# Decay gates of gated linear attention kept feature-major, logarithms two heads at a time, chunk sums by scans on VectorE

## The chip, the cores and the metric

One core of one Trainium2 chip runs the whole program. The metric is the time of one execution on the device in microseconds (us), as the median of three runs. Beside it one execution was taken by the hardware profiler; its span is the time from the first to the last instruction of the profile.

## What is computed

The kernel computes two two-layer transformer blocks on 256 tokens of width 1024 in float32. The first has a forgetting-gate attention layer, a latent attention layer and two squared-relu feed-forward layers; the second has a gated linear attention layer (GLA), a short-convolution layer and two convolutional feed-forward layers. The change touches only the GLA mixer, and in it only the decay gates:

```python
def gla_mixer(h, w_in, w_gate_up, b_gate, head_norm_g, w_out):   # 4 heads, key dim 128, value dim 256
    q, k, v, g, a_low = split(h @ w_in)                           # a_low: 16 columns
    log_a = log_sigmoid(a_low @ w_gate_up + b_gate) / 16          # 512 gates for each token
    bcum = cumsum(log_a, inside chunks of 64 tokens)
    q_in = q * 128 ** -0.5 * exp(bcum)
    k_in = k * exp(-bcum)
    k_dec = k * exp(b_last - bcum)                                # b_last: bcum at the chunk's end
    # masked scores q_in k_in inside a chunk, k_dec carries the state to the next chunk
```

The kernel has log_sigmoid(z) as min(z, 0) - ln(1 + exp(min(z, -z))).

## The kernel before, in words

**Matrix products.** Activations stand feature-major (features on partitions, 256 tokens in the free direction). Every weight matrix arrives from memory in chunks of 256 columns into four raw slots (`w_raw`). A chunk is two halves of 128 columns. For each half ScalarE rounds the raw weights into `w_hi` (line 1344), VectorE computes the remainder `w_lo` (line 1753), and TensorE makes 24 matrix products with them (lines 782 to 784, or 814 to 816 where tokens are to stand on partitions). A helper called `prep` does this on ScalarE and on VectorE, three halves ahead of the half that TensorE is at. `w_hi` and `w_lo` have room for four halves, so ScalarE's `prep` waits until TensorE has finished the half that lies four before. TensorE waits for `w_lo` before each half (`split_ready`), and in the GV stage before each pair of halves, since each token block there uses both halves of a chunk.

**Order.** Each engine executes its own list in the written order; semaphores tie the lists together. The stages around the change are GA (the 16 low-rank gate columns), GQK (8 halves, queries and keys), GV (8 token blocks over 8 halves, values), GG (8 halves, output gate) and GO. What is not a matrix product of a stage is written between the halves at fixed places: "if n == 3" is after the evacuation of half 3 of the stage.

**The decay gates before.** Behind GQK half 2 TensorE makes the gate product token-major, one 512-column product for each block of 128 tokens (line 1208). On VectorE, behind GQK half 3, for each token block the bias is added (line 2159, from a copy of the bias on all partitions, `g_bias`) and min(z, -z) is taken (line 2160). ScalarE, at GQK step 4 between two `prep`s, takes exp and then ln(1 + .) of all 1024 columns at once (lines 1627 and 1629). VectorE behind GQK half 6 forms the logarithm of the decay (line 2165). Behind token block 0 of GV TensorE forms the sums inside chunks, feature-major, by eight float32 products with a triangular matrix (`gla_cum`, line 1216); they land in the two PSUM banks `score`. ScalarE makes exp of them and of their negatives (lines 1635 and 1638). VectorE forms the differences to the chunk ends (lines 2180 to 2187), ScalarE their exponentials (lines 1652 and 1653), and VectorE multiplies keys and queries by them (lines 2192 to 2202).

VectorE evacuates each half of GQK from PSUM with one operation (`scaled`, line 1931). ScalarE evacuates the GV blocks in pairs (line 1646).

Lines in the profile are lines of the kernel before.

Of the kernel before, what the change touches and what calls it, by code (L numbers as in the profile page):

```python
# [78 lines left out]
for _name, _n in [("mix0", 8), ("ffn0", 8), ("kv", 8), ("mix1", 8), ("ffn1", 8), ("final1", 8), ("mix2", 8),  # L79
                  ("ffn2", 8), ("mix3", 8), ("ffn3", 8), ("final2", 8), ("kv_a", 2), ("q_a", 3), ("head", 8),  # L80
                  ("sc_conv", 24), ("conv0", 132), ("conv1", 132)]:
    VEC[_name] = N_VEC
    N_VEC += _n
# [7 lines left out]
for _name, _n in [("ones", 128), ("ident", 128), ("mask", 256), ("tri_chunk", 128), ("cos", 256),  # L91
                  ("sin", 256), ("tile_mask", 128), ("pick", FOX_H),
                  ("head_row", 3 * 32 + P), ("eps", 1)]:
    CON[_name] = N_CON
    N_CON += _n


def shape_constants():

    con = np.zeros((P, N_CON), np.float32)  # L100
    at = lambda name, n: con[:, CON[name]:CON[name] + n]
    i = np.arange(P)
    at("ones", 128)[:] = 1.0
    at("ident", 128)[:] = np.eye(P)

    at("mask", 256)[:, 128:] = np.where(i[None, :] <= i[:, None], 0.0, MASKED)

    same = (i[:, None] // GLA_C) == (i[None, :] // GLA_C)
    upto = i[:, None] <= i[None, :]
    at("tri_chunk", 128)[:] = np.where(same & upto, 1.0 / GATE_TAU, 0.0)  # L110
# [12 lines left out]
    return con  # L123


def build(nc, io):
    ctx = ExitStack()
    with ctx:
# [93 lines left out]
        g_z = sb("g_z", [P, TT, 512])  # L222
        g_e = sb("g_e", [P, TT, 512])
# [17 lines left out]
        g_bias = sb("g_bias", [P, 512])  # L241
# [26 lines left out]
        tri_chunk = con[:, CON["tri_chunk"]:CON["tri_chunk"] + 128]  # L268
# [245 lines left out]
        def _(sp):  # L514
# [80 lines left out]
            sp.dma_start(g_bias[:], io["gla_b_gate_2"][0:1, :].partition_broadcast(P)).then_inc(gla_small_landed, 16)  # L595
# [52 lines left out]
        def _(pool):  # L648
# [94 lines left out]
            for h in range(GLA_H):  # L743
                pool.wait_ge(gla_act, 15 + 4 * h)
                nc.gpsimd.tensor_tensor(tmp_of(2 * h), tmp_of(2 * h), tmp_of(2 * h + 1), ALU.add).then_inc(head_sq, 1)
# [12 lines left out]
        def _(pe):  # L758
# [469 lines left out]
            def gla_scores(t):  # L1228

                pe.wait_ge(gla_dve, 11)  # L1230
# [15 lines left out]
            def gla_out(n):  # L1246

                h = n // 2
                e = slice(n * P, (n + 1) * P)
                bank_ = gla_bank[n % 4]  # L1250
                if n == 0:
                    pe.wait_ge(act_evac, AE["GV"] + 8)
                    pe.wait_ge(gla_act, 11)
                    pe.wait_ge(gla_dve, 13)
                if n >= 4:
                    pe.wait_ge(gla_act, 11 + 2 * (n - 4) + 2)
                nc.tensor.matmul(bank_[:, 0:T], g_v[:, 0, e], g_sT[:, h, 0:2, :], start=True, stop=False)
                step(nc.tensor.matmul(bank_[:, P:T], g_v[:, 1, e], g_sT[:, h, 2, :], start=False, stop=True))

            def gla_stat():  # L1260

                pe.wait_ge(gla_act, 27)
                for h in range(GLA_H):
                    pe.wait_ge(head_sq, h + 1)
                    last = nc.tensor.matmul(misc[:, 0:T], head_row[:, 32 * (3 - h):32 * (3 - h) + P], tmp_of(2 * h), start=h == 0,
                                            stop=h == GLA_H - 1)
                step(last)

            def gla_spread():

                pe.wait_ge(gla_dve, 15)
# [56 lines left out]
        def _(act):  # L1328
# [292 lines left out]
            for n in range(8):  # L1621
# [3 lines left out]
                if n == 4:  # L1625
                    act.wait_ge(gla_dve, 2)
                    step(nc.scalar.activation(g_e[:], g_e[:], ACT.Exp))
                    act.wait_ge(gla_act, 1)
                    step(nc.scalar.activation(g_e[:], g_e[:], ACT.Ln, bias=1.0))
            prep(C0["GV"], 0)  # L1630
            for g in range(2):
                act.wait_ge(gla_pe, 3 + g)
                hs = slice(2 * g, 2 * g + 2)
                v = score[g][:].rearrange("p (h t) -> p h t", h=2)
                step(nc.scalar.activation(g_eb[:, hs, :], v, ACT.Exp))
                v = v.rearrange("p h (t c s) -> p h t c s", t=TT, c=2)
                for c in range(2):
                    step(nc.scalar.activation(key_tiles(c)[:, hs], v[:, :, :, c, :], ACT.Exp, scale=-1.0))
            for n in range(8):
# [10 lines left out]
                if n == 1:  # L1650
                    act.wait_ge(gla_dve, 6)
                    step(nc.scalar.activation(g_kk[:, :, K_X:K_X + P], g_kk[:, :, K_X:K_X + P], ACT.Exp))
                    step(nc.scalar.activation(far_keys(), far_keys(), ACT.Exp))
# [3 lines left out]
                if n == 6:  # L1657
                    act.wait_ge(gla_pe, 7)
# [10 lines left out]
            for n in range(8):  # L1669
                if n < 7:  # L1670
                    prep(C0["GG"] + n // 2, n % 2)
                if n in (1, 2):
                    for m in range(4 * (n - 1), 4 * (n - 1) + 4):
                        act.wait_ge(gla_pe, 8 + m)
                        if m == 0:
                            act.wait_ge(gla_dve, 11)
                        step(nc.scalar.activation(g_o[:, m, :], gla_bank[m % 4][:, 0:T], ACT.Copy, scale=gain("head", m)))
                        step(nc.scalar.activation(tmp_of(m), gla_bank[m % 4][:, 0:T], ACT.Square))
                if n == 3:
                    act.wait_ge(gla_dve, 14)  # L1680
# [64 lines left out]
        def _(dve):  # L1745
# [421 lines left out]
            def near_scores(t):  # L2167
                dve.wait_ge(gla_zeroed, 1)
                dve.wait_ge(gla_pe, 5 + t)
# [3 lines left out]
            for n in range(8):  # L2173
                prep(C0["GV"] + n // 2, n % 2)
                if n == 0:
                    for g in range(2):
                        dve.wait_ge(gla_act, 5 + 3 * g)
# [21 lines left out]
                if n == 3:  # L2199
                    dve.wait_ge(gla_act, 10)  # L2200
# [13 lines left out]
            def head_norm(m):  # L2214

                dve.wait_ge(gla_pe, 17 + m // 2)
# [7 lines left out]
            for n in range(8):  # L2224
# [6 lines left out]
                if n == 3:  # L2231
                    dve.wait_ge(gla_act, 28)
# [6 lines left out]
                if n == 2:  # L2239
                    dve.wait_ge(gla_pe, 16)  # L2240
# [69 lines left out]
            "ffn_w_up", "ffn_w_down", "gla_w_in_2", "gla_b_gate_2", "gla_w_out_2", "sc_w_in_2",  # L2310
# [35 lines left out]
```

## Time and profile before

| what | value |
|---|---|
| median of 3 runs | 1117.34 us (1117.2 to 1117.8) |
| the profiled execution | 1117.06 us |
| its span | 1115.3 us |
| TensorE busy in the span | 1109.2 us (99%) |
| VectorE busy | 851.9 us (76%) |
| ScalarE busy | 664.5 us (60%) |
| GpSimd busy | 252.9 us (23%) |
| DMA queue of the weights | 201.90 MB, 56.0% of 16 engines' span |

In the profile PE is TensorE's matrix products and PEld its weight loads, DVE is VectorE, ACT ScalarE, POOL GpSimd, SP the engine that issues the transfers. Matrix products overlap: each is shown with its whole latency, so the time that one costs is the distance between the starts of neighbours. In a timeline a line holds the start, the duration, the engine, the source line, the operation, what it writes and reads, how many instructions were merged into it, and in brackets the idle time before it with what ended that.

### The profile page before, as it was taken

Reading aid. Unit: us, or ns where it says so; the run is one execution under the profiler, and the core shown is the slowest. Engines: PE = TensorE matmul, PEld = TensorE weight load, DVE = VectorE, ACT = ScalarE, POOL = GpSimd, SP = SyncE. Lnnn points to the kernel's source line nnn. Section 1 sums busy time; section 2 is a strip of 40 time slices with the busy share of each in tenths; the row PEclk is TensorE's granted clock in tenths of the full one; section 3 lists DMA queues with packets and bytes.
Section 4 is the critical chain, followed back from the end, with each engine's and each line's share of the span. In section 5 each row is a group of like instructions: output and inputs, shape, how many; then the busy total and the mean of one; then the engine's idle time right before and its main releaser. Section 6 shows DMA issues by size and latency. Waiting matters only on the chain.

```text
span 1115.3 us, 26109 instructions
## 1 busy us (share of the span) xinstructions
PE 1109.2 (99%) x9634; PEld 1093.9 (98%) x9634; DVE 851.9 (76%) x1373; ACT 664.5 (60%) x1113; POOL 252.9 (23%) x248
## 2 busy tenths in 40 slices
PE   9999999999999999999999999999999999999998
PEld 9999999999998999999999999999999999999998
DVE  7866877666686977756577699999658888999854
ACT  7666666545577656644466566666455456666544
POOL 0002300001140500011200364544211034444421
PEclk9999999999999999999999999999999999999999
DMA  9533755555652765565464455654666565655461
GB/s 336 191 130 114 227 188 188 190 196 179 170 180 77 223 193 188 178 202 193 150 195 146 152 188 166 205 196 141 207 205 226 173 216 169 201 200 179 150 213 62
DMA packets 206799, 203.02 MB, mean 182 GB/s; under 512 B 9824, under 2 KB 204896, under 8 KB 206736
## 3 DMA queue, kind: packets, MB, share of 16 engines
q1 hardware_dynamic: 206592, 201.90, 56.0%
q8 instruction: 42, 0.69, 0.3%
q10 hardware_dynamic: 144, 0.26, 0.1%
q14 instruction: 21, 0.17, 0.0%
HBM read 201.10 MB, written 1.05 MB: 181 GB/s over the span
## 4 chain that ended last, share of the span: by engine, by line
PE 99%; DVE 0%; issue 0%; ACT 0%; DVEq 0%
PE gemm L782 29%; PE gemm L784 29%; PE gemm L783 29%; PE gemm L814 2%; PE gemm L815 1%; PE gemm L816 1%; PE gemm L791 1%; PE gemm L793 1%; PE gemm L792 1%; PE score L1015 1%; PE gemm L1027 1%; PE score L1147 0%; PE misc L1052 0%; PE misc L844 0%; PE gemm L1163 0%; PE score L1235 0%
## 5 line engine op out<-in xcount | busy, mean ns | idle before, releaser
L1753 DVE TENSOR_TENSOR w_lo<-w_raw,w_hi 128x1024 fp32r<-128x1024 f32 (+2 forms) x401 | 478.9, 1200 | 140.7 <-ACT w_hi L1344 138.8
L1344 ACT CAST w_hi<-w_raw 128x1024 fp32r<-128x1024 f32 (+2 forms) x401 | 400.4, 1004 | 141.8 <-PE gemm L784 136.4
L782 PE MATMUL gemm<-act_a,w_hi 128*128 128x256 f32 (+1 forms) x1688 | 466.6, 276 | 0.0
L784 PE MATMUL gemm<-act_a,w_lo 128*128 128x256 f32 (+1 forms) x1688 | 464.6, 275 | 0.0
L783 PE MATMUL gemm<-act_a,w_hi 128*128 128x256 f32 (+1 forms) x1688 | 464.5, 275 | 0.0
L782 PEld LDWEIGHTS gemm<-act_a,w_hi 128*128 128x128 f32 (+1 forms) x1688 | 316.2, 187 | 2.1 <-issue 1.8
L783 PEld LDWEIGHTS gemm<-act_a,w_hi 128*128 128x128 f32 (+1 forms) x1688 | 316.2, 187 | 0.3
L784 PEld LDWEIGHTS gemm<-act_a,w_lo 128*128 128x128 f32 (+1 forms) x1688 | 316.1, 187 | 0.2
L782 PE MATMUL gemm<-hid,w_hi 128*128 128x256 f32 x864 | 238.2, 276 | 0.0
L784 PE MATMUL gemm<-hid,w_lo 128*128 128x256 f32 x864 | 237.7, 275 | 0.0
L783 PE MATMUL gemm<-hid,w_hi 128*128 128x256 f32 x864 | 237.7, 275 | 0.0
L783 PEld LDWEIGHTS gemm<-hid,w_hi 128*128 128x128 f32 x864 | 162.2, 188 | 0.1
L782 PEld LDWEIGHTS gemm<-hid,w_hi 128*128 128x128 f32 x864 | 162.2, 188 | 0.1
L784 PEld LDWEIGHTS gemm<-hid,w_lo 128*128 128x128 f32 x864 | 162.2, 188 | 0.0
L661 POOL TENSOR_TENSOR sqt<-x 128x256 f32<-128x256 f32 x47 | 54.0, 1149 | 274.7 <-DVE x L1810 190.1
L684 POOL TENSOR_TENSOR tmp<-tmp,tmp 128x256 f32<-128x256 f32 x44 | 67.9, 1543 | 119.5 <-DVE tmp L1885 119.5
L1433 ACT ACTIVATE tmp<-tmp,vec 128x256 f32<-128x256 f32 x88 | 44.9, 511 | 77.7 <-DVE tmp L1870 72.6
L1394 ACT ACTIVATE tmp<-gemm 128x256 f32<-128x256 f32 x64 | 24.6, 384 | 59.3 <-PE gemm L784 59.3
L782 PE MATMUL gemm<-act_b,w_hi 128*128 128x256 f32 x216 | 59.6, 276 | 0.0
L784 PE MATMUL gemm<-act_b,w_lo 128*128 128x256 f32 x216 | 59.4, 275 | 0.0
L783 PE MATMUL gemm<-act_b,w_hi 128*128 128x256 f32 x216 | 59.4, 275 | 0.0
L1885 DVE SCALAR_TENSOR_TENSOR tmp<-tmp,vec,tmp 128x254 f32<-128x254 f32 x88 | 47.7, 542 | 12.7 <-DVE tmp L1882 1.8
(302 smaller groups left out, 1427.7 us busy)
## 6 DMA issues: line engine op xcount, KB each, us to landing
w_raw<-in_ffn_w_up SPq DMA_DIRECT2D x76, 1024.0 KB, 5.2
w_raw<-in_ffn_w_down SPq DMA_DIRECT2D x32, 1024.0 KB, 5.2
w_raw<-in_gla_w_in SPq DMA_DIRECT2D x12, 1024.0 KB, 5.1
w_raw<-in_ffn_w_down SPq DMA_DIRECT2D x16, 768.0 KB, 4.5
w_raw<-in_sc_w_in SPq DMA_DIRECT2D x12, 1024.0 KB, 5.2
w_raw<-in_fox_w_in SPq DMA_DIRECT2D x10, 1024.0 KB, 7.3
w_raw<-in_ffn_w_down SPq DMA_DIRECT2D x16, 640.0 KB, 4.2
w_raw<-in_fox_w_out SPq DMA_DIRECT2D x4, 1024.0 KB, 5.1
```

The costliest lines, as they stand in the source:

```text
L661: nc.gpsimd.tensor_tensor(sqt[:], tile, tile, ALU.mult).then_inc(pool_sq, 1)
L684: nc.gpsimd.tensor_tensor(y, y, tmp2[:, n % 2, :], ALU.mult).then_inc(gated_ready, 1)
L782: nc.tensor.matmul(ps, wh[:, k, cols], act[:, k0 + k, 0, :], start=start and k == 0, stop=False)
L783: nc.tensor.matmul(ps, wh[:, k, cols], act[:, k0 + k, 1, :], start=False, stop=False)
L784: last = nc.tensor.matmul(ps, wl[:, k, cols], act[:, k0 + k, 0, :], start=False, stop=stop and k == nk - 1)
L791: nc.tensor.matmul(ps, wh, act[:, k, 0, :], start=k == 0, stop=False)
L814: nc.tensor.matmul(ps, act[:, k, 0, tok], wh(k), start=k == 0, stop=False)
L1344: nc.scalar.copy(split_half(w_hi, nc_, nj), raw_half(nc_, nj)).then_inc(w_hi_ready, 1)
L1394: nc.scalar.activation(tmp[:, n % 4, :], bank_of(stage, n)[:, 0:T], ACT.Relu).then_inc(act_evac, 1)
L1433: nc.scalar.activation(tmp[:, n % 4, :], tmp2[:, 2 + n % 2, :], ACT.Copy, scale=w).then_inc(tap_ready, 1)
L1753: nc.vector.tensor_tensor(split_half(w_lo, nc_, nj), raw_half(nc_, nj), split_half(w_hi, nc_, nj).bitcast(F32), ALU.subtract).then_inc(w_l ...
L1885: nc.vector.scalar_tensor_tensor(out=y[:, 2:T], in0=u[:, 0:T - 2], scalar=w0, in1=y[:, 2:T], op0=ALU.mult, op1=ALU.add).then_inc(conv_done, 1)
```

## The change

The gate product is made feature-major: four products of 256 tokens, one for each head, into the two `score` banks. The bias is then a column of `vec` and no longer a broadcast copy, and its transfer goes. Minimum and exp and ln are taken for two heads at a time, so ScalarE's order becomes exp, ln, exp, ln on 512 columns each. The triangular matrix, its eight products and `gla_cum` go; in their place VectorE runs one scan for each head over 256 tokens. The scan multiplies the running sum by a row `chunk_start` that is 0 at the first token of each chunk and 1 elsewhere, which restarts it. The division by 16 goes into the scale of the later exponentials. Those now read `g_e` in SBUF in place of the `score` banks. The VectorE work is spread: decay logarithm and scan of head 0 behind GQK half 5, scan of head 1 and decay logarithm of heads 2 and 3 behind half 6, scans of heads 2 and 3 behind half 7. The constants' tensor grows by 128 columns and `vec` by 4. All other hunks only renumber semaphore values.

```diff
@@ TensorE
-                pe.wait_ge(gla_small_landed, 32)
-                for t in range(TT):
-                    r = slice(32 * t, 32 * t + GATE_RANK)
-                    step(nc.tensor.matmul(score[t][:, 0:512], g_aT[r, t * P:(t + 1) * P], g_up[r, :], start=True, stop=True))
-
-            def gla_cum():
-
-                pe.wait_ge(gla_dve, 4)
-                for g in range(2):
-                    for h in range(2 * g, 2 * g + 2):
-                        for t in range(TT):
-                            last = nc.tensor.matmul(score[g][:, (h % 2) * T + t * P:(h % 2) * T + (t + 1) * P],
-                                                    g_z[:, t, h * P:(h + 1) * P], tri_chunk, start=True, stop=True)
-                    step(last)
+                pe.wait_ge(gla_small_landed, 16)
+                for h in range(GLA_H):
+                    r = slice(32 * (h % 2), 32 * (h % 2) + GATE_RANK)
+                    last = nc.tensor.matmul(score[h % 2][:, h // 2 * T:h // 2 * T + T], g_up[r, h * P:(h + 1) * P], g_aT[r, :],
+                                            start=True, stop=True)
+                    if h >= 2:
+                        step(last)
...
                 token_half("GV", n, act_a, act_evac, AE["GV"])
-                if n == 0:
-                    gla_cum()
@@ ScalarE
                 if n == 4:
-                    act.wait_ge(gla_dve, 2)
-                    step(nc.scalar.activation(g_e[:], g_e[:], ACT.Exp))
-                    act.wait_ge(gla_act, 1)
-                    step(nc.scalar.activation(g_e[:], g_e[:], ACT.Ln, bias=1.0))
+                    for g in range(2):
+                        hs = slice(2 * g, 2 * g + 2)
+                        act.wait_ge(gla_dve, 1 + g)
+                        step(nc.scalar.activation(g_e[:, hs, :], g_e[:, hs, :], ACT.Exp))
+                        act.wait_ge(gla_act, 1 + 2 * g)
+                        step(nc.scalar.activation(g_e[:, hs, :], g_e[:, hs, :], ACT.Ln, bias=1.0))
             prep(C0["GV"], 0)
             for g in range(2):
-                act.wait_ge(gla_pe, 3 + g)
+                act.wait_ge(gla_dve, 5 + 3 * g)
                 hs = slice(2 * g, 2 * g + 2)
-                v = score[g][:].rearrange("p (h t) -> p h t", h=2)
-                step(nc.scalar.activation(g_eb[:, hs, :], v, ACT.Exp))
+                v = g_e[:, hs, :]
+                step(nc.scalar.activation(g_eb[:, hs, :], v, ACT.Exp, scale=1.0 / GATE_TAU))
@@ VectorE
             def bcum(g):
-                return score[g][:].rearrange("p (c s) -> p c s", s=GLA_C)
+                return g_e[:, 2 * g:2 * g + 2, :].rearrange("p h (c s) -> p (h c) s", s=GLA_C)
+
+            def log_decay(g):
+                hs = slice(2 * g, 2 * g + 2)
+                step(nc.vector.scalar_tensor_tensor(out=g_z[:, hs, :], in0=g_z[:, hs, :], scalar=0.0, in1=g_e[:, hs, :],
+                                                    op0=ALU.min, op1=ALU.subtract), wait=True)
+
+            def chunk_sums(h):
+                step(nc.vector.tensor_tensor_scan(g_e[:, h, :], chunk_start, g_z[:, h, :], 0.0, ALU.mult, ALU.add))
...
                 if n == 3:
-                    for t in range(TT):
-                        dve.wait_ge(gla_pe, 1 + t)
-                        dve.wait_ge(gla_small_landed, 32)
-                        link(nc.vector.tensor_tensor(g_z[:, t, :], score[t][:], g_bias[:], ALU.add))
-                        step(nc.vector.scalar_tensor_tensor(out=g_e[:, t, :], in0=g_z[:, t, :], scalar=-1.0, in1=g_z[:, t, :],
-                                                            op0=ALU.mult, op1=ALU.min))
+                    for h in range(GLA_H):
+                        dve.wait_ge(gla_pe, 1 + h % 2)
+                        last = nc.vector.tensor_scalar(g_z[:, h, :], score[h % 2][:, h // 2 * T:h // 2 * T + T], gain("gate", h), None,
+                                                       ALU.add)
+                        if h % 2:
+                            link(last)
+                            hs = slice(h - 1, h + 1)
+                            step(nc.vector.scalar_tensor_tensor(out=g_e[:, hs, :], in0=g_z[:, hs, :], scalar=-1.0, in1=g_z[:, hs, :],
+                                                                op0=ALU.mult, op1=ALU.min))
+                if n == 5:
+                    dve.wait_ge(gla_act, 2)
+                    log_decay(0)
+                    chunk_sums(0)
                 if n == 6:
-                    dve.wait_ge(gla_act, 2)
-                    for t in range(TT):
-                        step(nc.vector.scalar_tensor_tensor(out=g_z[:, t, :], in0=g_z[:, t, :], scalar=0.0, in1=g_e[:, t, :],
-                                                            op0=ALU.min, op1=ALU.subtract))
+                    chunk_sums(1)
+                    dve.wait_ge(gla_act, 4)
+                    log_decay(1)
+                if n == 7:
+                    chunk_sums(2)
+                    chunk_sums(3)
```

Here `link` waits for the end of the instruction before, `step` counts one up on a semaphore, and `step(..., wait=True)` also waits for it.

## Rows read from the trace of the kernel before

**Rows 1.** The page: engines' busy time, and TensorE's granted clock in 40 slices.

```profile
PE 1109.2 (99%) x9634; PEld 1093.9 (98%) x9634; DVE 851.9 (76%) x1373; ACT 664.5 (60%) x1113; POOL 252.9 (23%) x248
...
PEclk9999999999999999999999999999999999999999
```

**Rows 2.** The waits of TensorE, first of two: us, times, longest.

```profile
PE misc L1052 <- DVE f_cum L1962: 1.2, 1, 1.2
```

**Rows 3.** Timeline of TensorE: gate product, GV token blocks and chunk sums.

```profile
565.03 1.13 PE L1208 MATMUL score<-g_up,g_aT 16*128 16x512 f32 x4
566.09 0.39 PE L782 MATMUL gemm<-act_a,w_hi 128*128 128x256 f32 x1
...
579.85 0.28 PE L814 MATMUL gemm<-w_hi,act_a 128*128 128x256 f32 x1
...
582.57 1.95 PE L1216 MATMUL score<-con,g_z 128*128 128x128 f32 x16
584.28 0.37 PE L814 MATMUL gemm<-w_hi,act_a 128*128 128x256 f32 x1
584.49 0.28 PE L815 MATMUL gemm<-w_hi,act_a 128*128 128x256 f32 x1
...
587.12 0.28 PE L814 MATMUL gemm<-w_hi,act_a 128*128 128x256 f32 x1
...
592.56 0.29 PE L814 MATMUL gemm<-w_hi,act_a 128*128 128x256 f32 x1
```

**Rows 4.** Timeline of VectorE in GQK, from the evacuation of half 3.

```profile
569.18 0.41 DVE L1931 TENSOR_TENSOR g_q<-gemm,rstd 128x256 f32<-128x256 f32 x1
569.52 0.68 DVE L2159 TENSOR_TENSOR g_z<-score,g_bias 128x512 f32<-128x512 f32 x1
570.23 0.69 DVE L2160 SCALAR_TENSOR_TENSOR g_e<-g_z 128x512 f32<-128x512 f32 x1
...
572.16 1.22 DVE L1753 TENSOR_TENSOR w_lo<-w_raw,w_hi 128x1024 fp32r<-128x1024 f32 x1
...
578.16 1.22 DVE L1753 TENSOR_TENSOR w_lo<-w_raw,w_hi 128x1024 fp32r<-128x1024 f32 x1
...
579.63 1.28 DVE L2165 SCALAR_TENSOR_TENSOR g_z<-g_z,g_e 128x512 f32<-128x512 f32 x2
```

**Rows 5.** Timeline of ScalarE at GQK step 4, and the rounding behind it.

```profile
570.24 1.28 ACT L1627 ACT_TABLE_LOAD   x1
572.28 1.06 ACT L1627 ACTIVATE g_e<-g_e 128x1024 f32<-128x1024 f32 x1 [0.76 <-DVE g_e L2160]
573.36 1.28 ACT L1629 ACT_TABLE_LOAD   x1
574.66 1.06 ACT L1629 ACTIVATE g_e<-g_e 128x1024 f32<-128x1024 f32 x1
575.62 2.93 ACT L1344 CAST w_hi<-w_raw 128x1024 fp32r<-128x1024 f32 x3
```

**Rows 6.** Timeline of VectorE in the first layer: a scan and its successor.

```profile
27.98 0.68 DVE L2017 TENSOR_TENSOR_SCAN f_exp<-con,f_z 16x256 f32<-16x256 f32 x1
28.59 0.38 DVE L1931 TENSOR_TENSOR f_q<-gemm,rstd 128x256 f32<-128x256 f32 x1
```

**Rows 7.** Timeline of VectorE in GV: first and last chunk-end operation, w_lo.

```profile
584.85 0.17 DVE L2180 COPY g_last<-score 128x8 f32<-128x8 f32 x1 [1.33 <-ACT g_kk L1638]
...
587.04 0.42 DVE L2187 TENSOR_TENSOR g_kk<-g_end,score 128x256 f32<-128x256 f32 x1
...
591.17 1.23 DVE L1753 TENSOR_TENSOR w_lo<-w_raw,w_hi 128x1024 fp32r<-128x1024 f32 x1 [0.16 <-ACT w_hi L1344]
```

**Rows 8.** Timeline of ScalarE in GV, step 1: exponential and next rounding.

```profile
589.04 0.64 ACT L1652 ACTIVATE g_kk<-g_kk 128x512 f32<-128x512 f32 x1
...
590.10 1.05 ACT L1344 CAST w_hi<-w_raw 128x1024 fp32r<-128x1024 f32 x1
```

**Rows 9.** The first matrix products of the program, by their source line (ns).

```profile
L1052 PE MATMUL misc<-f_cum x22: 283/415/579, 1.2 to 5.8; 128*128 128x256 f32 x22
```

More of the change, by code:

```diff
@@ L80 @@
                   ("ffn2", 8), ("mix3", 8), ("ffn3", 8), ("final2", 8), ("kv_a", 2), ("q_a", 3), ("head", 8),
-                  ("sc_conv", 24), ("conv0", 132), ("conv1", 132)]:
+                  ("sc_conv", 24), ("conv0", 132), ("conv1", 132), ("gate", GLA_H)]:
     VEC[_name] = N_VEC
@@ L90 @@
 N_CON = 0
-for _name, _n in [("ones", 128), ("ident", 128), ("mask", 256), ("tri_chunk", 128), ("cos", 256),
+for _name, _n in [("ones", 128), ("ident", 128), ("mask", 256), ("chunk_start", 256), ("cos", 256),
                   ("sin", 256), ("tile_mask", 128), ("pick", FOX_H),
@@ L106, in shape_constants @@
     at("mask", 256)[:, 128:] = np.where(i[None, :] <= i[:, None], 0.0, MASKED)
-    same = (i[:, None] // GLA_C) == (i[None, :] // GLA_C)
     upto = i[:, None] <= i[None, :]
-    at("tri_chunk", 128)[:] = np.where(same & upto, 1.0 / GATE_TAU, 0.0)
+    at("chunk_start", 256)[:] = np.where(np.arange(T) % GLA_C == 0, 0.0, 1.0)[None, :]
     at("tile_mask", 128)[:] = np.where(upto, 1.0, 0.0)
@@ L221, in build @@
         g_v = sb("g_v", [P, TT, D])
-        g_z = sb("g_z", [P, TT, 512])
-        g_e = sb("g_e", [P, TT, 512])
+        g_z = sb("g_z", [P, GLA_H, T])
+        g_e = sb("g_e", [P, GLA_H, T])
         g_eb = sb("g_eb", [P, GLA_H, T])
@@ L240, in build @@
         g_up = sb("g_up", [GATE_ROWS, 512])
-        g_bias = sb("g_bias", [P, 512])
         s_c = sb("s_c", [P, 2, T])
@@ L267, in build @@
         mask = con[:, CON["mask"]:CON["mask"] + 256]
-        tri_chunk = con[:, CON["tri_chunk"]:CON["tri_chunk"] + 128]
+        chunk_start = con[:, CON["chunk_start"]:CON["chunk_start"] + 256]
         cos_t = con[:, CON["cos"]:CON["cos"] + 256]
@@ L743, in _ @@
             for h in range(GLA_H):
-                pool.wait_ge(gla_act, 15 + 4 * h)
+                pool.wait_ge(gla_act, 17 + 4 * h)
                 nc.gpsimd.tensor_tensor(tmp_of(2 * h), tmp_of(2 * h), tmp_of(2 * h + 1), ALU.add).then_inc(head_sq, 1)
@@ L1228, in gla_scores @@
             def gla_scores(t):
-                pe.wait_ge(gla_dve, 11)
+                pe.wait_ge(gla_dve, 15)
                 for h in range(GLA_H):
@@ L1252, in gla_out @@
                     pe.wait_ge(act_evac, AE["GV"] + 8)
-                    pe.wait_ge(gla_act, 11)
-                    pe.wait_ge(gla_dve, 13)
+                    pe.wait_ge(gla_act, 13)
+                    pe.wait_ge(gla_dve, 17)
                 if n >= 4:
-                    pe.wait_ge(gla_act, 11 + 2 * (n - 4) + 2)
+                    pe.wait_ge(gla_act, 13 + 2 * (n - 4) + 2)
                 nc.tensor.matmul(bank_[:, 0:T], g_v[:, 0, e], g_sT[:, h, 0:2, :], start=True, stop=False)
@@ L1260, in gla_stat @@
             def gla_stat():
-                pe.wait_ge(gla_act, 27)
+                pe.wait_ge(gla_act, 29)
                 for h in range(GLA_H):
@@ L1269, in gla_spread @@
             def gla_spread():
-                pe.wait_ge(gla_dve, 15)
+                pe.wait_ge(gla_dve, 19)
                 for h in range(GLA_H):
@@ L1625, in _ @@
                 if n == 4:
-                    act.wait_ge(gla_dve, 2)
-                    step(nc.scalar.activation(g_e[:], g_e[:], ACT.Exp))
-                    act.wait_ge(gla_act, 1)
-                    step(nc.scalar.activation(g_e[:], g_e[:], ACT.Ln, bias=1.0))
+                    for g in range(2):
[4 more added lines that the diff above has]
+                        step(nc.scalar.activation(g_e[:, hs, :], g_e[:, hs, :], ACT.Ln, bias=1.0))
             prep(C0["GV"], 0)
             for g in range(2):
-                act.wait_ge(gla_pe, 3 + g)
+                act.wait_ge(gla_dve, 5 + 3 * g)
                 hs = slice(2 * g, 2 * g + 2)
-                v = score[g][:].rearrange("p (h t) -> p h t", h=2)
-                step(nc.scalar.activation(g_eb[:, hs, :], v, ACT.Exp))
+                v = g_e[:, hs, :]
+                step(nc.scalar.activation(g_eb[:, hs, :], v, ACT.Exp, scale=1.0 / GATE_TAU))
                 v = v.rearrange("p h (t c s) -> p h t c s", t=TT, c=2)
                 for c in range(2):
-                    step(nc.scalar.activation(key_tiles(c)[:, hs], v[:, :, :, c, :], ACT.Exp, scale=-1.0))
+                    step(nc.scalar.activation(key_tiles(c)[:, hs], v[:, :, :, c, :], ACT.Exp, scale=-1.0 / GATE_TAU))
             for n in range(8):
@@ L1650, in _ @@
                 if n == 1:
-                    act.wait_ge(gla_dve, 6)
-                    step(nc.scalar.activation(g_kk[:, :, K_X:K_X + P], g_kk[:, :, K_X:K_X + P], ACT.Exp))
-                    step(nc.scalar.activation(far_keys(), far_keys(), ACT.Exp))
+                    act.wait_ge(gla_dve, 10)
+                    step(nc.scalar.activation(g_kk[:, :, K_X:K_X + P], g_kk[:, :, K_X:K_X + P], ACT.Exp, scale=1.0 / GATE_TAU))
+                    step(nc.scalar.activation(far_keys(), far_keys(), ACT.Exp, scale=1.0 / GATE_TAU))
                 if n == 2:
@@ L1657, in _ @@
                 if n == 6:
-                    act.wait_ge(gla_pe, 7)
+                    act.wait_ge(gla_pe, 5)
                     act.wait_ge(gla_zeroed, 1)
@@ L1673, in _ @@
                     for m in range(4 * (n - 1), 4 * (n - 1) + 4):
-                        act.wait_ge(gla_pe, 8 + m)
+                        act.wait_ge(gla_pe, 6 + m)
                         if m == 0:
-                            act.wait_ge(gla_dve, 11)
+                            act.wait_ge(gla_dve, 15)
                         step(nc.scalar.activation(g_o[:, m, :], gla_bank[m % 4][:, 0:T], ACT.Copy, scale=gain("head", m)))
@@ L1679, in _ @@
                 if n == 3:
-                    act.wait_ge(gla_dve, 14)
+                    act.wait_ge(gla_dve, 18)
                     step(nc.scalar.activation(g_std, g_var, ACT.Sqrt))
@@ L2176, in _ @@
                     for g in range(2):
-                        dve.wait_ge(gla_act, 5 + 3 * g)
+                        dve.wait_ge(gla_act, 7 + 3 * g)
                         hs = slice(2 * g, 2 * g + 2)
@@ L2199, in _ @@
                 if n == 3:
-                    dve.wait_ge(gla_act, 10)
+                    dve.wait_ge(gla_act, 12)
                     step(nc.vector.tensor_tensor(g_kk[:, :, K_B:K_B + T], g_kk[:, :, K_B:K_B + T], g_k[:], ALU.mult))
@@ L2214, in head_norm @@
             def head_norm(m):
-                dve.wait_ge(gla_pe, 17 + m // 2)
+                dve.wait_ge(gla_pe, 15 + m // 2)
                 if m < KD - 1:
@@ L2231, in _ @@
                 if n == 3:
-                    dve.wait_ge(gla_act, 28)
+                    dve.wait_ge(gla_act, 30)
                     step(nc.vector.reciprocal(g_rec, g_std))
@@ L2239, in _ @@
                 if n == 2:
-                    dve.wait_ge(gla_pe, 16)
+                    dve.wait_ge(gla_pe, 14)
                     step(nc.vector.tensor_scalar(g_var, misc[:, 0:T], 1.0 / GLA_DV, EPS, ALU.mult, ALU.add))
```

7 lines of the change are left out of this document (3 added, 4 removed).

## The prediction

> **What bounds the kernel.** I read the page first: TensorE is busy 99% of the span, and its granted clock is full in every slice [rows 1]. Then the list of who waits for whom, for TensorE alone. It has only two entries, and the longer is 1.2 us at the very start [rows 2]. So TensorE sets the end, and a change can do only two things to the time: give TensorE more or less to do, or make it wait where it did not. The reader should see in the timelines how much it was from waiting in the region of the change. That is the distance from the moment when the second w_lo of a GV pair is finished to the moment when TensorE takes it. For halves 0 and 1 of GV the second remainder runs 578.16 to 579.38 [rows 4] and TensorE starts the block at 579.85 [rows 3]: 0.47 us to spare. For halves 4 and 5 it runs 591.17 to 592.40 [rows 7] and TensorE starts at 592.56 [rows 3]: 0.16 us to spare. Both pairs hang on a rounding that ScalarE does behind its exp and ln work. This is the place to cost with care.
>
> **TensorE's own work.** The sixteen records of the chunk sums begin at 582.57, and the next GV product at 584.28, 1.71 us later. The product behind that begins 0.21 later where neighbours elsewhere stand 0.113 apart (48 from 587.12 to 592.56, which is 5.44 / 48), so another 0.10 goes [rows 3]. Removing the sums gives **-1.81 us**.
>
> The gate product has 1024 columns before and after, as two products of 512 and then four of 256, each again two records. Now it takes 1.06 us to the next product [rows 3]. Four records of 512 columns in 1.06 us overlap in pairs: 128 columns cost 0.107 (1.71 / 16), so 512 would cost 0.43 alone, and four of them 1.71. The new form also alternates the two groups of rows, so I take no change. If it did not overlap it would cost 1.71, which is +0.65; if it overlapped better, 0.86, which is -0.20.
>
> **VectorE behind GQK half 3.** A 128x256 operation out of PSUM lasts 0.41 and lets the next start after 0.34; a 128x512 one lasts 0.69 [rows 4] and lets the next start after 0.61 (with the 0.03 of a link, 570.23 to 572.16 is twice 0.61 plus one 0.71). New: 0.34 + 0.41 + 0.03, then the minimum at 570.30, finished at 570.99; the second pair is done at 572.38, and the block takes 2.78 in place of 2.64. The +0.14 delays only the w_lo of the last GQK half, which TensorE takes some five microseconds later, and so costs nothing.
>
> **ScalarE at GQK step 4.** Here the cost arises. Before there is one table load (1.28) ahead of exp and one between exp and ln [rows 5]. With the order exp, ln, exp, ln there are four loads. The first is finished at 571.52, behind the first minimum (570.99), so exp of heads 0 and 1 starts at 571.54. A 128x512 activation lasts about 0.62 (0.64 in [rows 8]), and 0.02 lies on both sides of a load. One step exp, load, ln, load is 0.62 + 0.02 + 1.28 + 0.02 + 0.62 + 0.02 + 1.28 + 0.02 = 3.88. The second exp starts at 575.42 and the second ln at 577.36. The next rounding follows 0.53 behind it (589.04 to 590.10 is two such steps [rows 8]), at 577.89. It starts at 575.62 before. So the roundings of GV halves 0 to 3 come **2.27 us later**. In terms: two loads of 1.28, two more activation starts (4 x 0.62 - 2 x 1.06 = 0.36), 0.09 of gaps, less the 0.74 by which the first exp starts sooner. Three roundings take 2.93 [rows 5], 0.94 from start to start: half 0 is rounded by 578.94, half 1 by 579.88.
>
> **VectorE behind GQK half 5.** w_lo of half 0 starts at 578.96 and lets the next start after 1.14; the evacuation takes 0.34; then the decay logarithm, waited for to its end (0.69 + 0.03); then the first scan. The only scan in the trace, 16x256, lasts 0.68 and lets the next operation start after 0.61 [rows 6]. The same 256 columns on 128 partitions should cost the same, since evacuations of 16 and 128 partitions differ little; bounds are 0.34 (a plain 128x256 operation) and 1.22, twice the row of the scan; I take the row itself. w_lo of half 1 then starts at 578.96 + 1.14 + 0.34 + 0.72 + 0.61 = 581.77 and is finished at 582.99. TensorE is ready at 579.85 and starts at 583.01: it **waits 3.16 us**. The work that was put between the two remainders (0.72 + 0.61) makes 1.33 of it, the late rounding the rest, less the 0.47 that there was to spare.
>
> **The next pairs.** VectorE goes on from 582.91: evacuation 0.34, scan 0.61, decay logarithm 0.72, w_lo of half 2 1.14, evacuation 0.34, two scans 1.22, then w_lo of half 3 from 587.28 to 588.50. TensorE ends its two blocks at 583.01 + 2 x 2.72 = 588.45, so this is a draw (+0.05). The chunk-end operations follow at 588.42 and take 2.61 for four heads, as now (584.85 to 587.46 [rows 7]), to 591.03. ScalarE is free for the key exponentials 1.92 behind the start of token block 2 (589.04 against 587.12 [rows 3, 8]), so at 590.42; now it waits until 591.06. Two steps of 0.53 later, at 592.12, it rounds half 5, until 593.17, and w_lo of half 5 is finished at 594.41. TensorE wants it 5.44 behind the start of block 2 (588.50), at 593.94: another **+0.47**. Behind that TensorE stands 1.85 later than before, and the same chains (the multiplications ahead of the scores, the remainders of halves 6 and 7) come to a few tenths ahead of its need, so nothing more is added.
>
> **What costs nothing.** The bias transfer goes, and the constants are 128 columns longer, 64 KB; TensorE waits for no transfer in the whole trace [rows 2] and the constants are used only far behind their issue. Exponentials read SBUF in place of PSUM, by the same number of columns. Weight chunks are requested later by the delay of w_lo, but a slot is filled four chunks before its use.
>
> **Sum.** -1.81 + 3.16 + 0.05 + 0.47 = +1.87 us. Against the profiled execution (1117.06, of which the span is 1115.3 and 1.76 lie around it) that is 1118.93; the median of before is 0.28 above that execution. I predict 1119.2. In a kernel where 0.2% (2.2 us) is what can be told from no change, that is no change, close to its upper edge. Bounds of the likeliest case: scans at the low bound (0.27 less), no second wait (0.47 less) and a better overlapped gate product (0.20 less) give +0.9; a scan at the high bound in the first gap (0.61 more) and a gate product without overlap (0.65 more) give +3.1. So 1118.2 to 1120.5.
>
> **Rival 1: the clock falls in the wait.** Granted clock is full in all slices of before [rows 1], but the trace holds no wait of over 1.2 us. Its first products show what a TensorE that has been idle does: 22 of 256 columns from 1.2 to 5.8, 0.22 us each [rows 9], against 0.113 later. That is the pace of the lower level, 1.2 GHz. If the wait of 3.16 us made it fall back for as long a stretch as at the start, 21 products would take 0.22 in place of 0.113, another 21 x 0.106 = +2.2: 1121.4. The wait is as long as nothing in this trace, which speaks for it; TensorE is full of work on both sides, which speaks against it. The Trainium skill ("TensorE: Matmul & The Clock Gate", Part 1) says that an idle TensorE drops to half rate and has to work for a while before it has the full one; no row of before shows a drop in mid-program.
>
> **Rival 2: no more table loads, so no wait.** If exp and ln could stay loaded together, ScalarE's step 4 would be shorter than now: first exp at 571.54, four activations, next rounding at about 574.0, so sooner than 575.62. Then even with 1.33 us more of VectorE work between the remainders of halves 0 and 1, w_lo of half 1 is done by about 579.5, in time, and only the -1.81 is left: 1115.5. This is the case on the other side. It decides if the rounding of half 0 starts before about 574.8. Against it stands that the trace has a load between exp and ln [rows 5], so the two are in different tables in this program. The Trainium skill ("ScalarE: Activation LUTs", Table sets: the hidden batching unit) lists a set with both, by which exp, ln, exp, ln would need one load; the trace disagrees with its load of 1.28 us between them.
>
> **Rival 3: the first wait alone.** If the second wait is not there, because the roundings have caught up, the sum is -1.81 + 3.16 = +1.35: 1118.7. It stays inside the likeliest case's range, but the trace after would tell.
>
> **Chances.** Two waits with the clock kept 0.52, the first alone 0.22, the clock falls 0.15, no added loads 0.05, something else 0.06 (half of it a longer delay that builds up). The part of the first two beyond 1119.6 is about 0.18, with rival 1 and the rest 0.36 slower. Faster by over 0.2% needs -2.2 us, more than the removal gives: 0.04. No change 0.60. The range from 1117.7 to 1121.5 leaves out rival 2, the low tail and the top of rival 1.
>
> **What would show it.** In the trace after: four table loads in the exp and ln lines between two GQK roundings, where there were two, the rounding of GV half 0 near 577.9; a scan of 128x256 at 0.68; TensorE's list of waits with one entry of about 3.2 us on w_lo at about 579.9 and one of about 0.5 at about 594; no product with the triangular matrix; the pace at 0.113 after the wait (0.22 would be rival 1). I am wrong if ScalarE loads fewer tables, if scans at 128 partitions cost far more, or if the later w_lo chain does not catch up.

## The result and the profile after

The changed kernel takes 1120.21 us as the median of 10 runs (1119.14 to 1120.62), against 1117.41 for the kernel before (10 runs). The ratio is 1.0023 with a 95% interval of 1.0015 to 1.0031, so the change costs about 2.8 us by the medians. The profiled execution took 1119.6 us with a span of 1117.8, which is 2.5 more than the span before. Line numbers in the fences below are those of each kernel: the three lines of the half products are L779 to L781 and L811 to L813 in the changed kernel, w_lo is L1743, the rounding L1332.

The list of TensorE's waits, where there were two rows before and none on w_lo [rows 2]:

```profile
PE gemm L811 <- DVE w_lo L1743: 3.0, 1, 3.0
PE misc L1049 <- DVE f_cum L1952: 1.2, 1, 1.2
PE gemm L1160 <- DVE m_q L1926: 0.3, 1, 0.3
```

The timeline of ScalarE in the changed kernel, to compare with [rows 5]. This trace runs 0.26 us ahead of the one before at the gate product, so 577.65 here is 577.91 there:

```profile
569.98 1.28 ACT L1617 ACT_TABLE_LOAD   x1
571.28 0.63 ACT L1617 ACTIVATE g_e<-g_e 128x512 f32<-128x512 f32 x1
571.93 1.28 ACT L1619 ACT_TABLE_LOAD   x1
573.22 0.63 ACT L1619 ACTIVATE g_e<-g_e 128x512 f32<-128x512 f32 x1
573.87 1.28 ACT L1617 ACT_TABLE_LOAD   x1
575.17 0.63 ACT L1617 ACTIVATE g_e<-g_e 128x512 f32<-128x512 f32 x1
575.82 1.28 ACT L1619 ACT_TABLE_LOAD   x1
577.11 0.63 ACT L1619 ACTIVATE g_e<-g_e 128x512 f32<-128x512 f32 x1
577.65 3.87 ACT L1332 CAST w_hi<-w_raw 128x1024 fp32r<-128x1024 f32 x4
```

Four loads stand where two stood, and the first rounding behind them is 2.29 us later (577.91 against 575.62). The timeline of VectorE, to compare with [rows 4]:

```profile
578.72 1.23 DVE L1743 TENSOR_TENSOR w_lo<-w_raw,w_hi 128x1024 fp32r<-128x1024 f32 x1 [4.85 <-ACT w_hi L1332]
579.86 0.42 DVE L1921 TENSOR_TENSOR g_k<-gemm,rstd 128x256 f32<-128x256 f32 x1
580.19 0.68 DVE L2142 SCALAR_TENSOR_TENSOR g_z<-g_z,g_e 128x512 f32<-128x512 f32 x1
580.91 0.69 DVE L2146 TENSOR_TENSOR_SCAN g_e<-con,g_z 128x256 f32<-128x256 f32 x1
581.52 1.20 DVE L1743 TENSOR_TENSOR w_lo<-w_raw,w_hi 128x1024 fp32r<-128x1024 f32 x1
```

VectorE stands idle for 4.85 us until the late rounding arrives. Before, it stood idle for 2.97 us at the same place:

```profile
576.69 1.23 DVE L1753 TENSOR_TENSOR w_lo<-w_raw,w_hi 128x1024 fp32r<-128x1024 f32 x1 [2.97 <-ACT w_hi L1344]
```

Then, in the changed kernel, a decay logarithm and a scan lie between the two remainders that TensorE needs. The second ends at 582.72. TensorE takes it at 582.77, and the timeline of TensorE shows what comes next:

```profile
579.48 0.28 PE L781 MATMUL gemm<-act_a,w_lo 128*128 128x256 f32 x1
582.77 0.58 PE L811 MATMUL gemm<-w_hi,act_a 128*128 128x256 f32 x1 [3.02 <-DVE w_lo L1743]
583.15 0.41 PE L812 MATMUL gemm<-w_hi,act_a 128*128 128x256 f32 x1
583.36 0.41 PE L813 MATMUL gemm<-w_lo,act_a 128*128 128x256 f32 x1
583.58 0.41 PE L811 MATMUL gemm<-w_hi,act_a 128*128 128x256 f32 x1
...
585.50 0.38 PE L811 MATMUL gemm<-w_hi,act_a 128*128 128x256 f32 x1
```

The starts are 3.29 apart over the wait, 3.18 more than the usual 0.113. Behind it they stand 0.21 apart instead of 0.113, which is the pace of the 1.2 GHz level, until 585.71 (14 starts). These 13 steps take 2.94 us in place of 1.47. The windows of the same trace give the granted clock as the third number from the end:

```profile
579.80:583.20 3.40, 0.43 (x2) 0.43 (x3) 3.37 (x7) 3.00 (x3) 0.00 (x0) 0.87 0.00 0
582.00:582.20 0.20, 0.00 (x0) 0.00 (x0) 0.20 (x1) 0.20 (x1) 0.00 (x0) 1.00 0.00 0
582.40:582.60 0.20, 0.00 (x0) 0.00 (x0) 0.20 (x1) 0.20 (x1) 0.00 (x0) 0.50 0.00 0
582.77:585.70 2.93, 2.93 (x13) 2.93 (x14) 2.90 (x5) 1.29 (x4) 0.00 (x0) 0.50 0.61 176
585.80:590.00 4.20, 4.20 (x39) 4.20 (x38) 4.03 (x12) 1.28 (x4) 0.00 (x0) 1.00 0.49 152
```

It is 0.50 behind the wait and 1.00 from 585.8 on. It falls inside the wait already: it is still 1.00 up to 582.2 and 0.50 from 582.4 on. The sum -1.81 + 3.18 + 1.47 = +2.84 fits the +2.80 of the medians. It fits the two traces too: their spans differ by 2.5, and the trace of the changed kernel was 0.26 ahead before the change began, which makes about 2.8. The page's line of the clock in 40 slices reads 9 throughout in both kernels; a stretch of 3 us is too short for it.

### The profile page after: what moved, and what is told of

The parts are those of the page before. It is cut to its first block, busy times and chain, and to the rows that moved or that the text cites. A ratio compares the mean times of both kernels' runs of the same rounds, so it can differ in the third digit from the quotient of the medians.

```text
span 1117.8 us, 26093 instructions
## 1 busy us (share of the span) xinstructions
PE 1108.7 (99%) x9622; PEld 1093.5 (98%) x9622; DVE 854.6 (76%) x1379; ACT 667.5 (60%) x1117; POOL 252.5 (23%) x248
## 4 chain that ended last, share of the span: by engine, by line
PE 99%; ACT 0%; DVE 0%; issue 0%; DVEq 0%; ACTq 0%
PE gemm L779 29%; PE gemm L781 29%; PE gemm L780 29%; PE gemm L811 2%; PE gemm L812 2%; PE gemm L813 2%; PE gemm L788 1%; PE gemm L790 1%; PE gemm L789 1%; PE score L1012 1%; PE gemm L1024 1%; PE score L1144 0%; PE misc L1049 0%; PE misc L841 0%; ACT w_hi L1332 0%; PE gemm L1160 0%
## 5 line engine op out<-in xcount | busy, mean ns | idle before, releaser
L1743 DVE TENSOR_TENSOR w_lo<-w_raw,w_hi 128x1024 fp32r<-128x1024 f32 (+2 forms) x401 | 478.9, 1200 | 141.8 <-ACT w_hi L1332 139.7
L1332 ACT CAST w_hi<-w_raw 128x1024 fp32r<-128x1024 f32 (+2 forms) x401 | 400.0, 1004 | 141.0 <-PE gemm L781 135.0
L779 PE MATMUL gemm<-act_a,w_hi 128*128 128x256 f32 (+1 forms) x1688 | 466.6, 276 | 0.0
L781 PE MATMUL gemm<-act_a,w_lo 128*128 128x256 f32 (+1 forms) x1688 | 464.5, 275 | 0.0
L779 PEld LDWEIGHTS gemm<-act_a,w_hi 128*128 128x128 f32 (+1 forms) x1688 | 316.2, 187 | 1.8 <-issue 1.4
L781 PEld LDWEIGHTS gemm<-act_a,w_lo 128*128 128x128 f32 (+1 forms) x1688 | 316.1, 187 | 0.2
L779 PE MATMUL gemm<-hid,w_hi 128*128 128x256 f32 x864 | 238.1, 276 | 0.0
L781 PE MATMUL gemm<-hid,w_lo 128*128 128x256 f32 x864 | 237.7, 275 | 0.0
L779 PEld LDWEIGHTS gemm<-hid,w_hi 128*128 128x128 f32 x864 | 162.2, 188 | 0.1
L781 PEld LDWEIGHTS gemm<-hid,w_lo 128*128 128x128 f32 x864 | 162.2, 188 | 0.0
L779 PE MATMUL gemm<-act_b,w_hi 128*128 128x256 f32 x216 | 59.6, 276 | 0.0
L781 PE MATMUL gemm<-act_b,w_lo 128*128 128x256 f32 x216 | 59.4, 275 | 0.0
```

The source lines that it names most:

```text
L779: nc.tensor.matmul(ps, wh[:, k, cols], act[:, k0 + k, 0, :], start=start and k == 0, stop=False)
L781: last = nc.tensor.matmul(ps, wl[:, k, cols], act[:, k0 + k, 0, :], start=False, stop=stop and k == nk - 1)
L1332: nc.scalar.copy(split_half(w_hi, nc_, nj), raw_half(nc_, nj)).then_inc(w_hi_ready, 1)
L1743: nc.vector.tensor_tensor(split_half(w_lo, nc_, nj), raw_half(nc_, nj), split_half(w_hi, nc_, nj).bitcast(F32), ALU.subtract).then_inc(w_l ...
```

## The experiments

Each kernel was timed in 11 runs beside the kernel before on the same chip. Its median there was 1117.43 us for the first four kernels and 1117.51 for the last three.

**Two table loads instead of four.** The changed kernel with this edit on ScalarE (and VectorE's first wait raised from 2 to 3):

```diff
                     for g in range(2):
                         hs = slice(2 * g, 2 * g + 2)
                         act.wait_ge(gla_dve, 1 + g)
                         step(nc.scalar.activation(g_e[:, hs, :], g_e[:, hs, :], ACT.Exp))
-                        act.wait_ge(gla_act, 1 + 2 * g)
+                    for g in range(2):
+                        hs = slice(2 * g, 2 * g + 2)
+                        act.wait_ge(gla_act, 1 + g)
                         step(nc.scalar.activation(g_e[:, hs, :], g_e[:, hs, :], ACT.Ln, bias=1.0))
```

> The changed kernel with ScalarE's order exp, exp, ln, ln in place of exp, ln, exp, ln; all else as in the changed kernel. My theory (two more table loads make the rounding of GV half 0 late): loads in step 4 fall from 4 to 2, the rounding starts near 575.4 in place of 577.65, w_lo of half 1 is finished about 580.5 where TensorE wants it at 579.6, so the wait falls from 3.0 us to about 0.9 us and the clock stays full: about 1116.5 us. If instead the VectorE work between the two remainders alone made the wait, it would stay above 1.3 us and the time above 1117. If the tables did not matter, the time stays at 1120.2.

Measured: 1117.02 us, ratio to the kernel before 0.9997 (0.9988 to 1.0006), which is 3.2 us less than the changed kernel. The timeline of ScalarE and the waits of TensorE in this kernel:

```profile
573.59 1.28 ACT L1621 ACT_TABLE_LOAD   x1
574.89 1.16 ACT L1621 ACTIVATE g_e<-g_e 128x512 f32<-128x512 f32 x2
575.95 2.93 ACT L1332 CAST w_hi<-w_raw 128x1024 fp32r<-128x1024 f32 x3
```

```profile
PE gemm L811 <- DVE w_lo L1745: 0.8, 1, 0.8
```

The rounding is early again and the wait is 0.81. Here only the logarithm and the scan between the two remainders are left as its cause. The kernel comes to 0.5 us above what I expected: a restart behind a wait costs a slow first step of 0.23, and 0.3 are lost ahead of token block 4, as in the next two kernels. The granted clock stays at 1.00 around the wait.

**The first scan behind half 6.** The changed kernel with

```diff
-                if n == 5:
+                if n == 6:
                     dve.wait_ge(gla_act, 2)
                     log_decay(0)
                     chunk_sums(0)
-                if n == 6:
                     chunk_sums(1)
                     dve.wait_ge(gla_act, 4)
                     log_decay(1)
```

> The changed kernel with the decay logarithm and scan of the first heads behind GQK half 6 in place of half 5, so nothing but the evacuation lies between the remainders of GV halves 0 and 1; four table loads stay. Theory of a debt that VectorE pays anyway: the first wait falls by 1.33 us to about 1.7, and 1.2 us of it comes back as a wait for half 3 before token block 2; no stretch at the lower clock, since neither wait is as long as 3 us: about 1118.9 us. If the clock falls in a wait of 1.7 us too, about 1120.2. If the late work is hidden, 1117.6.

Measured: 1119.32 us, ratio 1.0020 (1.0011 to 1.0029). The timeline of TensorE shows three waits, at token blocks 0, 2 and 4:

```profile
581.86 0.38 PE L811 MATMUL gemm<-w_hi,act_a 128*128 128x256 f32 x1 [1.71 <-DVE w_lo L1743]
582.08 0.28 PE L812 MATMUL gemm<-w_hi,act_a 128*128 128x256 f32 x1
...
588.57 0.39 PE L811 MATMUL gemm<-w_hi,act_a 128*128 128x256 f32 x1 [0.98 <-DVE w_lo L1743]
...
594.51 0.38 PE L811 MATMUL gemm<-w_hi,act_a 128*128 128x256 f32 x1 [0.20 <-DVE w_lo L1743]
```

As the theory of a debt has it, the wait is 1.3 shorter at block 0 and 1.0 of it comes back at block 2. No product runs at 0.21 behind a wait of 1.71: the clock is kept. The waits together are 2.89, close to the 3.02 of the changed kernel, and the time is 0.9 us less. Two of the eleven runs took 1120.3 and 1120.8 us with a granted clock of 1.0 over the whole; what made them longer is open.

**The wait filled with products.** The changed kernel with

```diff
             for n in range(8):
+                if n == 0:
+                    for _ in range(26):
+                        nc.tensor.matmul(trans[:, 0:T], act_a[:, 0, 0, 0:P], act_a[:, 0, 0, :], start=True, stop=True)
                 token_half("GV", n, act_a, act_evac, AE["GV"])
```

> The changed kernel with 26 products of 256 columns into a bank that is unused there, placed ahead of token block 0 of GV; they take about 26 x 0.113 = 2.94 us of the 3.0 us in which TensorE waited, and their result is not used. Theory that the fall of the clock costs 1.4 us beside the wait: no product behind the wait at 0.21 us, time 1118.8, less than the changed kernel although more is computed. If the stretch at the lower clock has another cause, or costs nothing, 1120.2 or a little more.

Measured: 1119.24 us, ratio 1.0017 (1.0008 to 1.0026), 0.97 less than the changed kernel though TensorE computes more. The timeline of TensorE:

```profile
579.67 3.24 PE L1269 MATMUL trans<-act_a 128*128 128x256 f32 x26
582.85 0.39 PE L811 MATMUL gemm<-w_hi,act_a 128*128 128x256 f32 x1
583.07 0.29 PE L812 MATMUL gemm<-w_hi,act_a 128*128 128x256 f32 x1
...
594.20 0.38 PE L811 MATMUL gemm<-w_hi,act_a 128*128 128x256 f32 x1
594.42 0.28 PE L812 MATMUL gemm<-w_hi,act_a 128*128 128x256 f32 x1
```

The first GV product starts as late as in the changed kernel (582.85 against 582.77), so the filling leaves the lateness of w_lo as it was and changes the clock; the products behind it keep a pace of 0.12. The gain is 0.97 and not 1.4 because a small stall comes up ahead of token block 4: the product at 594.20 starts 0.43 behind its predecessor, 0.3 more than usual. In the changed kernel the stretch at the lower clock brings TensorE to this block only at 595.15, when w_lo of its second half is finished (594.99), and no such stall is there.

**Fewer sums on TensorE.** The kernel before with

```diff
-                    for h in range(2 * g, 2 * g + 2):
-                        for t in range(TT):
+                    for h in range(2 * g, 2 * g + 1):
+                        for t in range(1):
```

> The kernel before with 2 of the 8 products with the triangular matrix (it leaves out three quarters of the sums inside chunks; the rest of the banks keeps the gate logits). It prices what the change takes from TensorE: 12 of 16 records at 0.107 us each, -1.3 us, so 1116.1 us; the whole removal would then be -1.7 to -1.8. If TensorE was waiting for something else there, less than 0.3 us.

Measured: 1115.99 us, ratio 0.9988 (0.9979 to 0.9997), -1.4 us. The timeline of TensorE, where four records take the place of the sixteen in [rows 3]:

```profile
582.54 0.61 PE L1216 MATMUL score<-con,g_z 128*128 128x128 f32 x4
582.91 0.37 PE L814 MATMUL gemm<-w_hi,act_a 128*128 128x256 f32 x1
583.11 0.28 PE L815 MATMUL gemm<-w_hi,act_a 128*128 128x256 f32 x1
```

From the sums to the next product it is 0.37 in place of 1.71. What TensorE is relieved of counts in full: 1.34 in the trace, 1.4 by the medians.

**No wait at all.** The changed kernel with this edit on ScalarE (and VectorE's first wait raised from 2 to 3):

```diff
             for n in range(8):
+                if n == 4:
+                    nc.scalar.preload_act_table(ACT.Exp)
                 prep(C0["GQK"] + n // 2, n % 2)
...
                 if n == 4:
-                    for g in range(2):
-                        ...
+                    act.wait_ge(gla_dve, 1)
+                    step(nc.scalar.activation(g_e[:, 0:2, :], g_e[:, 0:2, :], ACT.Exp))
+                if n == 5:
+                    act.wait_ge(gla_dve, 2)
+                    step(nc.scalar.activation(g_e[:, 2:4, :], g_e[:, 2:4, :], ACT.Exp))
+                    for g in range(2):
+                        hs = slice(2 * g, 2 * g + 2)
+                        act.wait_ge(gla_act, 1 + g)
+                        step(nc.scalar.activation(g_e[:, hs, :], g_e[:, hs, :], ACT.Ln, bias=1.0))
```

> The changed kernel with ScalarE's work laid out otherwise: the table of exp loaded ahead of the rounding of GQK step 4, the exp of heads 0 and 1 behind that rounding, the rounding of GV half 0 behind it, then the exp of heads 2 and 3 and both ln. My theory (the whole loss is TensorE's wait for w_lo of GV half 1, and the sums' removal is a gain of 1.8): w_lo of half 1 finished near 578, no wait of TensorE for a w_lo, 1115.6 us. If the scans cost time even when no remainder is late (VectorE is busier), 1116.5 or more. If only the number of loads matters, it is that of e1_two_loads, 1117.0.

Measured: 1115.51 us, ratio 0.9982 (0.9973 to 0.9991), -2.0 us: faster than the kernel before and 4.7 us faster than the changed one. The timelines of ScalarE and of VectorE:

```profile
571.46 0.64 ACT L1617 ACTIVATE g_e<-g_e 128x512 f32<-128x512 f32 x1 [0.95 <-DVE g_e L2166]
572.23 1.05 ACT L1332 CAST w_hi<-w_raw 128x1024 fp32r<-128x1024 f32 x1
573.18 0.62 ACT L1620 ACTIVATE g_e<-g_e 128x512 f32<-128x512 f32 x1
573.82 1.28 ACT L1624 ACT_TABLE_LOAD   x1
575.12 1.16 ACT L1624 ACTIVATE g_e<-g_e 128x512 f32<-128x512 f32 x2
576.18 1.04 ACT L1332 CAST w_hi<-w_raw 128x1024 fp32r<-128x1024 f32 x1
```

```profile
574.33 1.22 DVE L1748 TENSOR_TENSOR w_lo<-w_raw,w_hi 128x1024 fp32r<-128x1024 f32 x1
...
577.25 1.23 DVE L1748 TENSOR_TENSOR w_lo<-w_raw,w_hi 128x1024 fp32r<-128x1024 f32 x1
```

Half 0 is rounded ahead of the logarithms, half 1 behind them, and the second remainder ends at 578.48, more than a microsecond before TensorE's need. The list of TensorE's waits names no w_lo. The same scans at the same places now cost nothing. The traces say so more exactly than the medians: from the start of the gate product to one and the same product of the GG stage it is 58.05 us before (565.03 to 623.08) and 56.25 here (565.31 to 621.56). That is -1.80, the price of the sums alone. So neither the feature-major gate product nor the dropped bias transfer adds anything that can be seen here.

**Four loads in the kernel before.** Its exp and ln taken in two halves, nothing else of the change (VectorE also waits for the new semaphore ahead of the decay logarithm):

```diff
-                    act.wait_ge(gla_dve, 2)
-                    step(nc.scalar.activation(g_e[:], g_e[:], ACT.Exp))
-                    act.wait_ge(gla_act, 1)
-                    step(nc.scalar.activation(g_e[:], g_e[:], ACT.Ln, bias=1.0))
+                    act.wait_ge(gla_dve, 1)
+                    nc.scalar.activation(g_e[:, 0, :], g_e[:, 0, :], ACT.Exp).then_inc(gate_half, 1)
+                    act.wait_ge(gate_half, 1)
+                    nc.scalar.activation(g_e[:, 0, :], g_e[:, 0, :], ACT.Ln, bias=1.0).then_inc(gate_half, 1)
+                    ... # the same for g_e[:, 1, :] with gla_dve, 2 and gla_act
```

> The kernel before with one part of the change alone: exp and ln taken in two halves, in the order exp, ln, exp, ln; gates token-major, chunk sums on TensorE. Theory that the loads delay the roundings: rounding of GV half 0 at 577.9, TensorE waits 1.8 us for w_lo of half 1, no lower clock as in e2_scans_later: 1119.3 us. If the loads cost only together with the scans, 1117.4.

Measured: 1119.27 us, ratio 1.0016 (1.0007 to 1.0025), +1.8 us. The waits of TensorE:

```profile
PE gemm L815 <- DVE w_lo L1758: 1.7, 1, 1.7
```

Its timeline of ScalarE, 0.22 us behind that of the kernel before at the gate product, so that the rounding stands at 577.91 as in the changed kernel:

```profile
578.13 3.87 ACT L1345 CAST w_hi<-w_raw 128x1024 fp32r<-128x1024 f32 x4
```

The four loads alone, without scans, make a wait of 1.72. With e2_scans_later that splits the 3.02 of the changed kernel: 1.7 from the late rounding, 1.3 from the logarithm and the scan between the remainders.

**The loads apart.** The changed kernel, the second half of the exp and ln work moved one step on:

```diff
                 if n == 4:
-                    for g in range(2):
+                    ... # exp, ln of heads 0 and 1
+                if n == 5:
+                    ... # exp, ln of heads 2 and 3
```

> The changed kernel, all four table loads kept, but exp and ln of heads 2 and 3 moved behind the next rounding (that of GV half 0), so that one rounding lies between the two pairs of loads. Theory that it is the lateness of the rounding and not the loads' time that costs: half 0 rounded at about 574, half 1 at 578.7, TensorE waits 1.3 us in place of 3.0, clock full: 1117.1 us. If the four loads cost whatever their place, 1120.2.

Measured: 1117.22 us, ratio 0.9998 (0.9989 to 1.0007), 3.0 less than the changed kernel with the same four loads. The waits of TensorE:

```profile
PE gemm L811 <- DVE w_lo L1746: 1.3, 2, 1.2
```

The timelines of ScalarE and of VectorE:

```profile
574.37 1.03 ACT L1332 CAST w_hi<-w_raw 128x1024 fp32r<-128x1024 f32 x1
```

```profile
580.26 1.22 DVE L1746 TENSOR_TENSOR w_lo<-w_raw,w_hi 128x1024 fp32r<-128x1024 f32 x1 [1.94 <-ACT w_hi L1332]
```

One rounding between the pairs of loads takes the wait at block 0 from 3.02 to 1.18. Half 0 is rounded early, so the logarithm and the scan are done while VectorE would be idle anyway; what is left of the wait comes from the rounding of half 1, for which VectorE stands idle for 1.94 us. So the same four loads cost more or less by which rounding they hold up.

## Why the prediction was right or wrong

The range held the time and the direction of the likeliest case was right. The likeliest size, 1119.2, was 1.0 us too low, and the case that came true is rival 1, to which I gave 0.15. That 1120.21 also lies inside the bounds of the likeliest case (1118.2 to 1120.5) is luck: I drew them so wide for slower scans and a gate product without overlap, and neither came. Rival 1 had the mechanism but not the size. Its 1121.4 is 1.2 too high, since it took 2.2 for the stretch at the lower clock where 1.47 was measured, and kept the 0.5 of the later waits that this stretch hides.

- **TensorE's own work, -1.81.** Right. The fewer-sums kernel gave 1.4 for three quarters of the records, and the kernel without a wait gave 2.0 for all by the medians and 1.80 in the traces. The gate product takes the same 1.06 from its start to the next product (564.77 to 565.83 in the changed kernel), as assumed.
- **Table loads.** Right, to 0.02 us: 2.27 predicted, 2.29 in the trace, and every change between exp and ln had its load of 1.28. Rival 2 did not come true. The Trainium skill ("ScalarE: Activation LUTs", Table sets: the hidden batching unit) lists a set with both functions; the loads in the trace show that it was not in use here.
- **The scan.** Right: 0.69 on 128 partitions against 0.68 on 16 [rows 6], the next start 0.61 later.
- **The wait for half 1.** Right: 3.16 predicted, 3.18 between the starts.
- **The draw at block 2 and the +0.47 ahead of block 4.** In the changed kernel neither wait is there, since TensorE comes later for the lower clock. In the kernel with the wait filled there is none at block 2 either, and the one ahead of block 4 is 0.3. The whole of that kernel is +1.8, against my sum of +1.87, which describes a kernel whose clock does not fall. That the two agree so well is in part luck: I took 0.2 too much for the later waits and left out the slow first step behind each wait, 0.1 twice, though the same step of 0.21 stands behind the sums in [rows 3].
- **The clock.** This is the step that failed: I took the fall for unlikely since TensorE is full of work on both sides of the wait. In the changed kernel it fell within the wait. It cost 1.47 us with the restart, less than the 2.2 that I took from the start of the program, because TensorE was at 0.21 for 13 steps and not 21. Filling the wait removes it. Of the ten timed runs nine list a granted clock of 0.997 or 0.998 over the whole; one lists 1.000 and is the fastest, 1119.14, which is where the filled kernel stands (1119.24). No trace of that run is kept, so whether its wait was shorter is not known.

Of the two waits that I called the likeliest, the first is there as I priced it and the second is not in the changed kernel. What the term for the first lacked is the clock that goes with it. The chances of faster, same and slower (0.04, 0.60, 0.36) leaned to "no change" by that same step. The medians differ by 0.25%, just over my bound of 0.2%, but the interval of the ratio (1.0015 to 1.0031) holds values on both sides of it.

## What to carry to other kernels

When one engine is busy all the time, the question for work moved to another engine is not how busy that engine is but how much room there is between its next hand-over and the moment of need: here 0.47 us, at a place where VectorE stood idle for 2.97 us shortly before. Function changes on ScalarE should be counted as loads and laid so that a hand-over lies between them: exp and ln grouped, and one rounding moved ahead, turned +2.8 us into -2.0 us with all the scans kept. And a wait of TensorE as long as the one seen here has to be priced at its length plus a stretch at the lower clock, as nine of ten runs paid it.

## What the runs showed of the hardware

I had not expected the clock to fall in a wait this short. In the trace of the changed kernel a wait of 3.02 us took TensorE to the lower level, before the wait was over and for 2.94 us behind it; one of its ten timed runs seems to have escaped this, with a granted clock of 1.000. Waits of 1.72, 1.71 followed by 0.98, and 1.18 did not: the granted clock of those stretches is 1.00. Where between 1.72 and 3.02 the change lies was not tried.

The idle time that the profile lists is shorter than what a wait costs. The wait of 1.71 parts two starts by 1.99 instead of 0.113, and the first step behind it is 0.22 instead of 0.113, so it costs 2.0. The slow first step is no mark of a wait: it is 0.22 behind the gate product too, where TensorE did not wait (565.83 to 566.05 in the changed kernel).
